# First attention: plain transposes of the exponentials, and inverse totals multiplied in after the values

## The reference

```python
def window_attention(q, k, v, k_ctx, v_ctx, sink):      # 8 query heads, 2 key heads, head_dim 64
    ...
        s_win = jnp.where(valid[None, None, None], s_win, -jnp.inf)
        s_ctx = jnp.einsum('bqkgd,bckd->bkgqc', q_i, k_ctx).astype(jnp.float32) * scale
        logits = jnp.concatenate([s_win, s_ctx, sink_logits(sink, s_win.shape[:-1])], axis=-1)
        p = jax.nn.softmax(logits, axis=-1)
        ...
        return (jnp.einsum('bkgqj,bjkd->bqkgd', p_win, v_i)
                + jnp.einsum('bkgqc,bckd->bqkgd', p_ctx, v_ctx))

def even_mixer(...):
    ...
    y = jnp.concatenate([fourier_mix(f_in), attn], axis=-1) @ w_out
```

## Time and profile before

| | us |
|---|---|
| median of 3 runs | 1202.65 |
| lowest and highest | 1198.71, 1203.48 |
| the profiled execution | 1203.04 |
| its span in the trace | 1201.2 |
| mean granted clock of TensorE, share of full | 0.981 |
| TensorE, VectorE, ScalarE, GpSimd busy | 1138.1, 817.4, 590.6, 81.9 |

### The profile page before, as it was taken

One profiled execution on the slowest core, in us unless ns is written; L12 is line 12 of the kernel. 1 busy time (PEld: TensorE's weight loads), 2 busy tenths in 40 slices (PEclk: granted clock), 3 DMA queues, 4 the chain that ended last, 5 costly groups with the idle time before them and its releaser, 6 DMA issues.

```text
span 1201.2 us, 24026 instructions
## 1 busy us (share of the span) xinstructions
PE 1138.1 (95%) x10281; PEld 1081.4 (90%) x10281; DVE 817.4 (68%) x1496; ACT 590.6 (49%) x1084; POOL 81.9 (7%) x100
## 2 busy tenths in 40 slices
PE   5888789999998999999989899999999999999999
PEld 2687689999997999999988788888999999999998
DVE  3784769898885767555674678788664665877543
ACT  2435555544544544454464467653234545655432
POOL 0000110000011000001100011112600001000000
PEclk9789999999999999999998999999999999999999
DMA  9751639899884556751643322332123464855520
GB/s 388 294 205 63 244 146 368 321 351 353 319 324 158 222 211 235 250 186 42 247 176 106 106 104 74 106 106 71 38 72 106 168 215 151 332 188 195 201 84 14
DMA packets 32362, 226.40 MB, mean 188 GB/s; under 512 B 3584, under 2 KB 4736, under 8 KB 5120
## 3 DMA queue, kind: packets, MB, share of 16 engines
q1 hardware_dynamic: 30528, 221.20, 49.5%
q10 hardware_dynamic: 1728, 3.67, 0.8%
HBM read 223.80 MB, written 1.05 MB: 187 GB/s over the span
## 4 chain that ended last, share of the span: by engine, by line
PE 85%; DVE 9%; ACT 4%; DMA 1%; issue 1%; POOL 0%; SPq 0%; POOLq 0%; DVEq 0%; ACTq 0%
PE bank L564 23%; PE bank L565 22%; PE bank L566 22%; DVE sb_wlo L1894 2%; PE bank L1044 2%; PE bank L689 2%; DVE sb_tmp L1920 1%; DVE sb_ring L1935 1%; PE bank L1035 1%; PE bank L582 1%; PE bank L1066 1%; DMA sb_ring<-in_ada 1%; PE bank L592 1%; PE bank L1232 1%; ACT sb_whi L1378 1%; PE bank L602 1%
## 5 line engine op out<-in xcount | busy, mean ns | idle before, releaser
L564 PE MATMUL bank<-sb_xh,sb_whi 128*128 128x256 f32 (+1 forms) x1496 | 426.1, 285 | 8.7 <-DVE sb_wlo L1894 6.6
L565 PE MATMUL bank<-sb_xl,sb_whi 128*128 128x256 f32 (+1 forms) x1496 | 417.7, 279 | 0.0
L566 PE MATMUL bank<-sb_xh,sb_wlo 128*128 128x256 f32 (+1 forms) x1496 | 417.5, 279 | 0.0
L1894 DVE TENSOR_TENSOR sb_wlo<-sb_ring,sb_whi 128x1024 fp32r<-128x1024 f32 (+1 forms) x197 | 239.2, 1220 | 139.5 <-ACT sb_whi L1378 139.1
L564 PEld LDWEIGHTS bank<-sb_xh,sb_whi 128*128 128x128 f32 (+1 forms) x1496 | 284.2, 190 | 17.0 <-issue 12.4
L565 PEld LDWEIGHTS bank<-sb_xl,sb_whi 128*128 128x128 f32 (+1 forms) x1496 | 284.6, 190 | 0.1
L566 PEld LDWEIGHTS bank<-sb_xh,sb_wlo 128*128 128x128 f32 (+1 forms) x1496 | 284.4, 190 | 0.0
L1378 ACT ACTIVATE sb_whi<-sb_ring 128x1024 fp32r<-128x1024 f32 (+1 forms) x197 | 206.7, 1053 | 86.9 <-PE bank L566 79.6
L1894 DVE TENSOR_TENSOR sb_wlo<-sb_more,sb_whi 128x1024 fp32r<-128x1024 f32 x108 | 131.1, 1223 | 64.7 <-ACT sb_whi L1378 64.7
L564 PE MATMUL bank<-sb_hh,sb_whi 128*128 128x256 f32 x608 | 168.4, 277 | 0.0
L566 PE MATMUL bank<-sb_hh,sb_wlo 128*128 128x256 f32 x608 | 167.8, 276 | 0.0
(11 more groups left out here) (376 smaller groups left out, 1802.5 us busy)
## 6 DMA issues: line engine op xcount, KB each, us to landing
sb_more<-in_w SPq DMA_DIRECT2D x34, 1024.0 KB, 6.2
sb_ring<-in_w SPq DMA_DIRECT2D x32, 1024.0 KB, 5.7
sb_ring<-in_adaT SPq DMA_DIRECT2D x26, 1024.0 KB, 7.4
sb_ring<-in_f SPq DMA_DIRECT2D x22, 1024.0 KB, 4.9
sb_more<-in_adaT SPq DMA_DIRECT2D x18, 1024.0 KB, 8.7
sb_ring<-in_gn SPq DMA_DIRECT2D x8, 1024.0 KB, 5.0
sb_ring<-in_gd SPq DMA_DIRECT2D x8, 1024.0 KB, 4.8
sb_ring<-in_up SPq DMA_DIRECT2D x8, 1024.0 KB, 6.3
```

The costliest lines, as they stand in the source:

```text
L564: te.matmul(out, wh, rh, start=start, stop=False, skip_group_check=skip)
L565: te.matmul(out, wh, rl, start=False, stop=False, skip_group_check=skip)
L566: return te.matmul(out, wl, rh, start=False, stop=stop, skip_group_check=skip)
L1894: ve.tensor_tensor(lo, x, hi.bitcast(F32), ALU.subtract).then_inc(*lo_dve.up(n))
```

## The change

`turn0` becomes eight plain transposes of the exponentials; it waits for ScalarE's exponentials instead of GpSimd's diagonals. GpSimd spreads each head's inverse total over 64 columns (`wide0`), and `values0` transposes that into the second half of the output's bank before it multiplies, so that the bank holds the unscaled outputs and, beside them, the inverses in the same layout. After both halves of a group, ScalarE copies the inverses to SBUF, VectorE multiplies them into the outputs (`over`), ScalarE copies the product to `ah`, and VectorE subtracts `ah` from it for `al`. Some engines' next steps stand behind these.

```diff
@@ sbuf
-        dg0 = sb("dg0", [128, 2, 2, 128])
+        wide0 = sb("wide0", [128, 2, 128])
@@ tensor_program: turn0, values0
                 for u in range(2):
-                    P.wait_ge(*pool.at("dg0", i))
+                    P.wait_ge(*act.at("exp", i, u))
                     ps = take(RA if i < 2 else RAS, ("pt", i, u), (act, ("pt", i, u)))
                     for k in range(4):
-                        end = te.matmul(ps[:, k * 128:(k + 1) * 128], SBs[:, i % 4, u, k * 128:(k + 1) * 128], dg0[:, i % 2, u, :], start=True, stop=True)
+                        end = te.transpose(ps[:, k * 128:(k + 1) * 128], SBs[:, i % 4, u, k * 128:(k + 1) * 128], ident)
...
                 if t == 0:
-                    take(RO, ("o", j), (dve, ("a", 4 + j)))
+                    take(RO, ("o", j), (dve, ("over", j)))
+                P.wait_ge(*pool.at("wide0", i))
+                te.transpose(ps_of(("o", j))[:, T + t * 128:T + (t + 1) * 128], wide0[:, i % 2, :], ident)
@@ scalar_program
                         A.wait_ge(*pe.at("pv", i - 3))
-                        sc.activation(ah[:, 4 + j, :], ps_of(("o", j))[:, 0:T], ACT.Copy).then_inc(*act.up(("ah", 4 + j)))
+                        sc.activation(temp(("over", j), (dve, ("over", j))), ps_of(("o", j))[:, T:2 * T], ACT.Copy).then_inc(*act.up(("inv", j)))
+                        A.wait_ge(*dve.at("over", j))
+                        sc.activation(ah[:, 4 + j, :], tv_of(("over", j)), ACT.Copy).then_inc(*act.up(("ah", 4 + j)))
@@ vector_program
                     if t == 1:
-                        lower0(4 + j, ("o", j))
+                        r = temp(("over", j), ("a", 4 + j))
+                        V.wait_ge(*act.at("inv", j))
+                        ve.tensor_tensor(r, ps_of(("o", j))[:, 0:T], ta_of(("over", j)), ALU.mult).then_inc(*dve.up(("over", j)))
+                        V.wait_ge(*act.at("ah", 4 + j))
+                        ve.tensor_tensor(al[:, 4 + j, :], r, ah[:, 4 + j, :].bitcast(F32), ALU.subtract).then_inc(*dve.up(("a", 4 + j)))
@@ gpsimd_program
-                total = st[:, 64 + 2 * i:66 + 2 * i].unsqueeze(2).to_broadcast([128, 2, 128])
+                total = st[:, 64 + 2 * i:66 + 2 * i].unsqueeze(2).to_broadcast([128, 2, 64])
...
                 if i > 1:
-                    G.wait_ge(*pe.at("pt", i - 2, 1))
-                gp.tensor_tensor(dg0[:, i % 2, :, :], ident.unsqueeze(1).to_broadcast([128, 2, 128]), total, ALU.mult).then_inc(*pool.up(("dg0", i)))
+                    G.wait_ge(*pe.at("pv", i - 2))
+                gp.tensor_tensor(wide0[:, i % 2, :].rearrange("p (u d) -> p u d", u=2), ones.rearrange("p (u d) -> p u d", u=2), total,
+                                 ALU.mult).then_inc(*pool.up(("wide0", i)))
```

More of the change, by code:

```diff
@@ L1483, in scalar_program @@
                         pr = SBs[:, i % 4, u, :]
-                        sc.activation(pr, pr, ACT.Exp, bias=st[:, 16 + n:17 + n], accum_out=st[:, 32 + n:33 + n]).then_inc(*act.up())
+                        sc.activation(pr, pr, ACT.Exp, bias=st[:, 16 + n:17 + n], accum_out=st[:, 32 + n:33 + n]).then_inc(*act.up(("exp", i, u)))
                         sc.activation(st[:, 48 + n:49 + n], C("sink", hd, hd + 1), ACT.Exp, bias=st[:, 16 + n:17 + n]).then_inc(*act.up(("e", i, u)))
```

## The result

The changed kernel takes 1208.32 us, the median of 9 executions (1205.31 to 1212.05); the kernel before took 1202.09 beside it (9 executions, 1195.11 to 1206.34). The ratio is **1.0059, with a 95% interval of 1.0040 to 1.0078**. That is 7.1 us slower (4.8 to 9.4), just over the half per cent that the prediction named as the least that can be told. The forecast was +5.7 us and 1208.3. The profiled execution took 1207.74 us.

What follows compares the result with a forecast made beforehand. It took first attention as bound by TensorE and ScalarE until about 125 us, then by VectorE's reductions with ScalarE. Terms -1.1 + 2.7 + 1.5 + 1.7 + 0.9 gave +5.7 us, median 1208.3, range 1203.5 to 1212.0.

Steps and rivals of the forecast that it cites:

- The turns, -1.1: First attention: one-pass transposes shorten three early turns on the path, each gain capped at 0.36 us by ScalarE; -1.1 us.
- Rival D: Turns: transposes go through twice like the matmuls and save nothing; +7.1 us, 1209.8, chance 0.08.
- Rival C: First attention: round trips are hidden and all eight turns count, so the kernel is faster; 1197.8, chance 0.07.
- The round trips, 3 x 0.91: Head groups: VectorE waits for ScalarE twice; product, copy and hand-over add 0.91 us in three groups on the chain, +2.7.
- The tail, +1.5: Before mixout: ScalarE's weight split waits for VectorE's last product, so 1.61 us becomes 3.09; +1.5 us.
- The first three parts: Attention stage and tail at full clock: turns, round trips and tail, -1.1 + 2.7 + 1.5 = +3.1 us.
- Values at half clock, +0.9: Late first attention: values L782, 1.09 us and on the chain, meet half clock; +0.9 us, bounds 0 and 1.1.
- Half clock at mixout, +1.7: Mixout's start: after a hole of about 5.5 us, 3.4 us of dense products at half clock; +1.7, bounds 0 and 2.2.
- Rival B: First attention: transposes let the clock drop at about 120 us, half clock until mixout; +9.0 us, 1211.7, chance 0.20.
- Rival A: Attention and mixout: the clock holds, so only +3.1 us remains; 1205.8, chance 0.20.

Runs made afterwards that it cites:

- the turns alone: Kernel before with the turn as plain transposes of the exponentials, without GpSimd's diagonals and the softmax's division: 1200.83 us, ratio 0.998.
- The round trip alone: Changed kernel with the turns again as plain two-pass matmuls, with the identity: 1210.6 us, ratio 1.0048.
- the high parts ahead: Changed kernel with ScalarE splitting all four units of mixout's first weights before it waits for the last `over`: 1208.84 us, ratio 1.0052.
- the new order: Kernel before with both VectorE reductions of an iteration ahead of the low parts (`lower0`): 1198.25 us, ratio 0.9976.
- fillers in all the holes: Changed kernel with idle matmuls ahead of scores (7), a turn (3), values (5) and mixout (9), all transposes kept: 1204.36 us, ratio 1.0012.
- the fillers ahead of mixout: Changed kernel with eleven idle matmuls on TensorE ahead of mixout's products: 1209.78 us, ratio 1.0044.
- the scaling on GpSimd: Kernel before with plain transposes, GpSimd multiplying a pair's exponentials in place by the inverse totals: 1204.93 us, ratio 1.002.
- the last run: Kernel before with both reductions ahead of `lower0` and five idle matmuls ahead of mixout: 1193.57 us, ratio 0.994.
- the changed kernel with a reduction ahead of each of a group's waits: Changed kernel, mixout's first weight unit moved ahead, one VectorE reduction before each of a group's two waits: 1200.82 us, ratio 0.9996.
- the changed kernel with both: Changed kernel with a reduction ahead of each of a group's waits, and the Fourier heads' `lower0` also behind a reduction: 1200.14 us, ratio 0.9978.

## Why the prediction was right, point by point

- **The turns, -1.1.** Right, 1.04 measured, and for the reason given: in the changed kernel the Fourier copy starts the moment the exponentials end. Rival D falls with 8 records to a pair. Rival C, which puts all eight turns on the path (7.3 us), falls with the turns alone, which gave 5.1 us at the very most by time and 0.4 by the marks.
- **The round trips, 3 x 0.91.** Right: 0.91 from product to subtraction at 120.66, 133.36 and 144.15, on the chain each time, and 0.91 more from the first group to the second than before. I had noted under rival C that each L2033 already waits for ScalarE; what I did not see is that this wait was the stage's bound in the kernel before, and that the order, not the round trip, was the thing to change.
- **The tail, +1.5.** Right: 3.04 against the 3.09 worked out, and 1.51 more than before's 1.53. The first three parts together are 3.2 against 3.1.
- **Values at half clock, +0.9.** Right: 1.98 us at 141.71 for 1.09, and 1.09 again with the holes filled. I had not named the stretch of 6.8 us at half clock ahead of it, which cost nothing only because TensorE was off the chain there.
- **Half clock at mixout, +1.7.** The sign was right and the size was not; this is the term of the sum that was mis-sized. I took 3.4 us at half from the window behind the hole of 2.07, as though every low stretch were as long as that one. Behind 5.43 us it lasted 6.8 us, of which 5.1 fell on products, and the opening grew by 25.01 - 21.87 = **+3.1**, beyond my bound of 2.2 as well. Not all of that is half clock. The first 24 products, up to 158.57, took 2.4 us longer than before's. The 168 behind them took 19.79 us for 19.04, so 0.75 more, one every 0.118 us where before's come every 0.113, although the granted clock is 1.00 there and TensorE never idle. The round trip alone and the run with the high parts ahead show that slower pace too, the openings of the others don't; its cause stays open, and the forecast had no term for it. By the marks the 1.4 us between +1.7 and +3.1 is what parts +5.7 from +7.2, and it moved the result over the half per cent that I had it sit just under. Other kernels here had 2.8 us of the opening at half clock behind a hole of 2.53, 3.25 behind 3.90, 5.8 behind 4.66, 4.0 behind 5.04 and 6.05 behind 5.93. Only roughly do long holes go with long stretches, and the rows before showed no hole as long as these.
- **Rival B.** Its time was nearly as good as the forecast's, but not its mechanism. From 119 to 127 us, with a turn by transposes at 120.30 and another just ahead at 115.35, the clock was 1.00; half clock came later, behind holes, and also with plain matmuls; with the holes filled and the transposes kept it never came. The rule of the Trainium skill that stood with it ("TensorE: Matmul & The Clock Gate", Part 4) is that transposes don't count as busy in the same way. No run here shows them lowering the clock by themselves, in groups of eight among other products. The fillers added matmuls as well as closing holes, and a turn by transposes is also shorter, so whether transposes weigh less than matmuls in some degree was not separated.
- **Rival A.** The clock did not hold, but the kernel with its holes filled is what this rival describes: 1.0012 measured, 1205.8 - 1202.65 = 3.1 us or 1.0026 predicted, which lies in the interval.

**What stays open.** In the profiled executions the changed kernel reached the stage 4.26 us earlier than the one before (table load 94.21 against 98.47) and yet ended 4.4 later; stage and opening give 5.8 of these 8.7. The other 2.8 lie behind L610, where the instructions are the same in all kernels here: that part took 1024.4 us in the trace of before and 1027.2 in the changed kernel's, and 1023.0 to 1028.1 in the fourteen traces, so one trace of each can't tell it from scatter. The earlier start is of that kind too: the code ahead of the stage is the same, and the mean granted clock from 0 to 94.2 us was 0.86 in the trace of before and 0.91 in the other. Of the 5.4 us that the new order takes from before's stage, 1.7 go to the opening's half clock, and what is left is within what the interval allows.

## What to carry to other kernels

When engines hand a result back and forth, look at what is queued behind each wait before you count instructions: putting two independent reductions ahead of a group's two waits shortened the stage by 4.5 us, where the faster turns had given 1.04. Time taken off TensorE where it wasn't the bound came back as holes, and in eight of the eleven traces without fillers mixout's opening behind such a hole (2.46 to 5.93 us) was 1.3 to 3.6 us longer; a few idle matmuls were a cheap repair. And where a forecast has such a low stretch, leave room in its range for one twice as long as the trace of before shows.

## What the runs showed of the hardware that I had not expected

- The scatter between executions of one kernel goes with TensorE's granted clock. The 35 runs of the kernel before beside "fillers in all the holes" had mean clocks of 0.976 to 0.986 and times of 1194.96 to 1206.46, and lie near a line of 0.8 us less for 0.001 more of clock (correlation -0.89). The changed kernel's nine had 0.969 to 0.976, median 0.973, where before's medians beside the experiments were 0.979 to 0.983: 6 thousandths or more, some 5 us by that line, against the 4.0 of the marks. The three stretches at half clock in its windows above (6.8, 3.4 and 6.8 us) are 8.5 us of lost clock in a span of 1205.6, 7 thousandths; the one stretch of the earlier trace rows that lies in before's attention is 1.4 thousandths.
- The same hole doesn't always have the same sequel. A hole of 2.07 us stands ahead of the first Fourier token products in all fourteen traces, behind the same instructions. In five of them (before, the high parts ahead, the fillers ahead of mixout, the scaling on GpSimd, the last run) some 3.4 us at half clock came with it, and the eight records took 3.5 to 3.65 us; in the other nine the clock stayed at 1.00 and they took 1.96 or 1.97.
- Of three holes of 2.46 us before mixout two were followed by half clock (the kernel before in the new order, the changed kernel with a reduction ahead of each of a group's waits) and one was not (the changed kernel with both), as the holes of 2.76 (the turns alone) and 3.13 (the kernel before) were not. With fillers ahead of mixout, half clock never came there, though in one of the three kernels a hole of 2.02 us was left. So the hole's length alone doesn't settle it.
- Dense fp32 products came at two paces while the granted clock was 1.00: one every 0.113 us in mixout's opening in eleven traces, one every 0.118 in three.
- A VectorE instruction of 0.16 us lasted 0.75 in all six places where a GpSimd product of 1.89 us was running, and each time ended 0.02 us behind it.
